# Stick-breaking attention on one core: logarithm sums over a high and a low part, scores asked for two pairs of heads ahead, pooling samples written as whole rows

## The chip, the cores and the metric

The kernel runs on one core of one Trainium2 chip, as one program. The metric is the device time of one execution in microseconds (us); lower is better. Six engines matter here: TensorE for matrix products (PE, and PEld for its weight loads), VectorE (DVE), ScalarE (ACT), GpSimd (POOL), SyncE (SP, which only issues transfers), and 16 DMA engines that all queues share.

## What is computed

One inference step of a two-layer hybrid decoder, for a prompt of 512 tokens and 8 single-token samples, all in float32. Each layer is a feed-forward half step, a mixing step and a second feed-forward half step. The change touches only the mixing step of the first layer: stick-breaking attention of 8 heads of 64 and a pooling mixer of 4 channel groups.

```python
z = einsum('bqhd,bkhd->bhqk', qb, kb) * scale + bias
log_1m = where(mask, log_sigmoid(-z), 0.0)
log_w = log_sigmoid(z) + cumsum(log_1m, axis=3, reverse=True) - log_1m
w = where(mask, exp(log_w), 0.0)
out = einsum('bhqk,bkhd->bqhd', w, vb)
```

The samples attend in the same way to 512 cached keys and values each, read through a page table. The pooling mixer also returns, for each sample, its last 15 pooling inputs (`pool_sample`).

## The kernel before

Stages follow each other: `in0`, `out0` (feed-forward), `evin` (the projection of layer 0), attention, `evout` (its output projection), and so on. All engines run their own queue in program order and meet only at semaphores. The order of the work is written out by hand, one function per engine: `even_sp`, `even_pe`, `even_act`, `even_dve`, `even_pool`.

Float32 weights are not multiplied as float32. Each weight block is split into a high part `WH` (fp32r, by ACT, line 2140) and a low part `WL` (by DVE, line 2318), and three fp32r products take the place of one float32 product. Attention before the change uses plain float32 products instead.

For one head `h` the causal scores are kept transposed and packed: block j (of 4) holds keys 128j to 128j+127 and queries from 128j on, so the blocks are 512, 384, 256 and 128 columns wide (`LEN`), 1280 in all (`CAUSAL`). A head goes through these steps:

- `score` (PE, 685): 4 products into PSUM; the two heads of a pair use the two halves of the array rows. `PS[0]` has room for one block of each head of a pair.
- `biased` (DVE, 1056): scale and bias, PSUM into `ZS`; POOL then masks the diagonal block (1223).
- `sized` (DVE, 1096) or, for heads 0 and 1, an Abs on ACT (890): |z| into `SP`.
- `decay` (ACT, 892 and 898): exp(-|z|). `log` (ACT, 902): ln(1 + that). Between Exp and Ln ACT loads a table (2164).
- `softplus` (DVE, 1062): max(z, 0) + logarithm.
- `sums` (PE, 791 and 794): for each key block i, one product with the triangle `TRI` and one with `ONES` for each later block, 10 products a head; the float32 products show in the trace as two instructions each. `PS[1]` has two buffers.
- `log_weights` (DVE, 1069): z minus the sum. `weights` (ACT, 906): exp. `values` (PE, 809): the product with V for a pair; ACT and DVE then make the high and low part of the result (952, 1100).

The main loop runs over pairs t = 0 to 3. On PE, before the change, one period takes the blocks of the scores of pair t+1 in turn with the sums of head 2t (`scores`, `sums`), then `values(t-1)` among them, then `values_past(t)` (660, the cached values of two samples), then `ada_step("head", 2t)` (1960, blocks of the modulation matrix), the sums of head 2t+1, and `ada_step("head", 2t+1)`. Before the loop, PE runs `sums_past` (715, 718), `scores_of_one` (the scores of head 1) and `ada_step("start", 0)`. `side(i, half)` puts small work between the products of the last `evin` units i = 22 to 27: `scores_past`, `pooled`, `turn_past` and the scores of head 0 (`first_scores`).

SP loads the weight blocks (1916), the modulation blocks `AW` for each `ada_step` (633, each once its buffer has been used), and writes the outputs K, the pooling rows and V (625 to 629). POOL issues the cached pages (1231): the values of samples 2q and 2q+1 once `values_past(q-1)` has used the two buffers `KV`.

## Time and profile before

| | |
|---|---|
| median of 3 runs | 2427.94 us (2426.88 to 2428.55) |
| the profiled execution | 2428.46 us, its span 2426.8 us |
| PE busy | 2382.4 us, 98% of the span |
| DVE, ACT, POOL busy | 1241.0, 994.5, 114.9 us |
| attention: from 563.15 us (`sums_past`) to 654.26 us (first product of `evout`) | 91.1 us |
| the chain that ended last, shares | PE 88%, DVE 5%, ACT 3%, DMA 2% |

The span is what the trace covers; 1.7 us of the execution lie around it. Times in the rows count from the span's start. In the timeline a row is start, duration, engine, line, operation, output and inputs, shapes and a count of merged instructions; "[1.05 <-DVE ZN L1164]" is the time for which the engine was idle before it and what ended that. A matmul's duration includes the way through the array, so the price of a product in a dense row of products is the distance from one start to the next.

### The profile page before, as it was taken

Reading aid. Unit: us, or ns where it says so; the run is one execution under the profiler, and the core shown is the slowest. Engines: PE = TensorE matmul, PEld = TensorE weight load, DVE = VectorE, ACT = ScalarE, POOL = GpSimd, SP = SyncE. Lnnn points to the kernel's source line nnn. Section 1 sums busy time; section 2 is a strip of 40 time slices with the busy share of each in tenths; the row PEclk is TensorE's granted clock in tenths of the full one; section 3 lists DMA queues with packets and bytes.
Section 4 is the critical chain, followed back from the end, with each engine's and each line's share of the span. In section 5 each row is a group of like instructions: output and inputs, shape, how many; then the busy total and the mean of one; then the engine's idle time right before and its main releaser. Section 6 shows DMA issues by size and latency. Waiting matters only on the chain.

```text
span 2426.8 us, 43808 instructions
## 1 busy us (share of the span) xinstructions
PE 2382.4 (98%) x18802; PEld 2183.8 (90%) x18802; DVE 1241.0 (51%) x1725; ACT 994.5 (41%) x1399; POOL 114.9 (5%) x232
## 2 busy tenths in 40 slices
PE   6999999999999999999999999999999999999998
PEld 5999999965699999999999999887777999999998
DVE  5533246755576333357523347755554758633245
ACT  5422235635456222346422245533223546522243
POOL 0000000122100000000000000012222100000000
PEclk9999999999999999999999999999999999999999
DMA  8555345785537653565754255544545456642254
GB/s 308 180 183 183 124 149 179 252 211 139 190 113 228 215 173 95 188 206 175 261 184 156 83 168 189 188 153 165 170 165 165 136 177 182 206 126 88 87 179 155
DMA packets 122660, 417.10 MB, mean 172 GB/s; under 512 B 23387, under 2 KB 27611, under 8 KB 122211
## 3 DMA queue, kind: packets, MB, share of 16 engines
q1 hardware_dynamic: 88962, 301.92, 39.1%
q10 hardware_dynamic: 18144, 62.03, 7.1%
q0 software_dynamic: 15360, 50.34, 6.3%
q8 instruction: 149, 2.44, 0.4%
q14 instruction: 45, 0.36, 0.0%
HBM read 390.84 MB, written 23.41 MB: 171 GB/s over the span
## 4 chain that ended last, share of the span: by engine, by line
PE 88%; DVE 5%; ACT 3%; DMA 2%; issue 1%; SPq 0%; ACTq 0%; POOL 0%; DVEq 0%; POOLq 0%
PE PS L2026 70%; PE PS L1425 3%; PE PS L1960 2%; DVE WL L2318 2%; PE PS L1990 2%; PE PS L1355 1%; ACT WH L2140 1%; DMA AFIRST<-in_w_ada 1%; PE PS L791 1%; PE PS L1309 1%; PE PS L1340 1%; PE PS L1350 1%; PE PS L753 1%; DMA RAW<-in_w_out 1%; PE PS L1321 1%
## 5 line engine op out<-in xcount | busy, mean ns | idle before, releaser
L2318 DVE TENSOR_TENSOR WL<-RAW,WH 128x1024 fp32r<-128x1024 f32 (+1 forms) x478 | 633.0, 1325 | 647.9 <-ACT WH L2140 647.2
L2026 PE MATMUL PS<-HH,WH 128*128 128x260 f32 x3432 | 796.6, 285 | 3.2 <-DVE QKVS L1119 1.8
L2026 PE MATMUL PS<-HH,WL 128*128 128x260 f32 x3432 | 786.5, 283 | 0.0
L2026 PE MATMUL PS<-HL,WH 128*128 128x260 f32 x3368 | 769.6, 283 | 0.0
L2140 ACT ACTIVATE WH<-RAW 128x1024 fp32r<-128x1024 f32 (+1 forms) x478 | 542.2, 1135 | 425.4 <-PE PS L2026 267.0
L2026 PEld LDWEIGHTS PS<-HH,WH 128*128 128x128 f32 x3432 | 569.9, 188 | 25.4 <-issue 16.8
L2026 PEld LDWEIGHTS PS<-HH,WL 128*128 128x128 f32 x3432 | 569.4, 188 | 0.0
L2026 PEld LDWEIGHTS PS<-HL,WH 128*128 128x128 f32 x3368 | 557.0, 188 | 0.6 <-issue 0.2
L2026 PE MATMUL PS<-GH,WH 128*128 128x260 f32 x1408 | 386.4, 285 | 0.9 <-DVE WL L2318 0.8
L2026 PE MATMUL PS<-GL,WH 128*128 128x260 f32 x1408 | 384.2, 283 | 0.0
L2026 PE MATMUL PS<-GH,WL 128*128 128x260 f32 x1408 | 383.5, 283 | 0.0
L2026 PEld LDWEIGHTS PS<-GH,WH 128*128 128x128 f32 x1408 | 259.0, 188 | 3.4 <-issue 1.8
L2026 PEld LDWEIGHTS PS<-GL,WH 128*128 128x128 f32 x1408 | 258.9, 188 | 0.2
L2026 PEld LDWEIGHTS PS<-GH,WL 128*128 128x128 f32 x1408 | 259.1, 188 | 0.0
L2263 ACT ACTIVATE GH<-SQ 128x260 fp32r<-128x260 f32 (+1 forms) x118 | 62.3, 528 | 376.5 <-DVE SQ L2488 376.5
L2488 DVE TENSOR_TENSOR SQ<-SG,PS 128x260 f32<-128x260 f32 (+1 forms) x118 | 65.6, 556 | 166.6 <-PE PS L2026 165.8
L2260 ACT ACTIVATE SG<-PS 128x260 f32<-128x260 f32 (+1 forms) x118 | 57.6, 488 | 217.3 <-PE PS L2026 215.6
L2477 DVE TENSOR_TENSOR GL<-SQ,GH 128x260 fp32r<-128x260 f32 (+1 forms) x118 | 66.3, 562 | 57.6 <-ACT GH L2263 56.9
L2026 PE MATMUL PS<-OGL,WH 128*128 128x260 f32 x256 | 69.6, 282 | 0.0
L1960 PE MATMUL PS<-AW,CSP 128*32 128x256 f32 x1024 | 67.0, 383 | 0.0
L1879 POOL DMA_DIRECT2D SR<-in_ret_past x32 | 18.2, 570 | 952.5 <-DVE WL L2318 929.0
L1960 PEld LDWEIGHTS PS<-AW,CSP 128*32 128x32 f32 x1024 | 30.4, 109 | 23.0 <-issue 2.3
(340 smaller groups left out, 2317.5 us busy)
## 6 DMA issues: line engine op xcount, KB each, us to landing
RAW<-in_w_in SPq DMA_DIRECT2D x236, 512.0 KB, 3.7
RAW<-in_w_out SPq DMA_DIRECT2D x120, 704.0 KB, 4.0
AW<-in_w_ada ACTq DMA_DIRECT2D x114, 512.0 KB, 5.5
RAW<-in_w_odd SPq DMA_DIRECT2D x60, 512.0 KB, 3.7
RAW<-in_w_odout SPq DMA_DIRECT2D x30, 512.0 KB, 3.9
RAW<-in_w_even SPq DMA_DIRECT2D x28, 512.0 KB, 4.0
KV<-in_v_pages POOLq DMA_DIRECT2D x32, 256.0 KB, 4.8
SR<-in_ret_past POOLq DMA_DIRECT2D x32, 256.0 KB, 4.0
```

Source lines behind the costliest of these rows:

```text
L753: last = nc.tensor.matmul(PS[tt // 2][:, tt % 2, :], src[k][:, tt // 2, (tt % 2) * P:(tt % 2 + 1) * P], w[:, w0:w0 + RV], start=(j + kk + ...
L791: last = nc.tensor.matmul(PS[1][:, i % 2, 0:LEN[i]], TRI[:], SP[h % 4][:, OFF[i]:OFF[i] + LEN[i]], start=True, stop=(i == 3))
L1425: last = nc.tensor.matmul(PS[tt // 2 if full else 0][:, tt % 2, :], src[k][:, tt // 2, (tt % 2) * P:(tt % 2 + 1) * P], w[:, w0:w0 + RV], s ...
L1960: last = nc.tensor.matmul(ADAP[CG * j:CG * j + CG, int(g == 1), 0:2 * P], CSP[:, k, :], w[:, 2 * P * j:2 * P * j + 2 * P], start=(k == 0), ...
L1990: last = nc.tensor.matmul(ps[:, x, 0:HT], w[:, k * P:(k + 1) * P], src[k][:, x, :], start=(start and k == 0), stop=(stop and k == KC - 1))
L2026: last = nc.tensor.matmul(ps[:, x, 0:HT], w[:, k * P:(k + 1) * P], src[k0 + k][:, x, :], start=(begin and t == 0), stop=(end and t == 2))
L2140: nc.scalar.activation(parts(p)[0], RAW[:, from_:from_ + w], ACT.Copy).then_inc(hi_done, 1)
L2260: nc.scalar.activation(SG[:, s, hs], PS[0][:, hs, 0:HT], ACT.Silu).then_inc(gate_evac, 1)
L2263: nc.scalar.activation(GH[:, r // 2, hs], G32[:, s, hs], ACT.Copy).then_inc(gh_done, 1)
L2318: nc.vector.tensor_tensor(low_, RAW[:, from_:from_ + w], high_.bitcast(F32), ALU.subtract).then_inc(lo_done, 1)
L2477: nc.vector.tensor_tensor(GL[:, r // 2, hs], G32[:, r // 2 % 2, hs], GH[:, r // 2, hs].bitcast(F32), ALU.subtract).then_inc(gl_done, 1)
L2488: nc.vector.tensor_tensor(G32[:, s, hs], SG[:, s, hs], PS[1][:, hs, 0:HT], ALU.mult).then_inc(up_evac, 1)
```

## The change

All of it is in the attention of layer 0 and the outputs written beside it.

```diff
-        ZS / SP: four buffers each, used by h % 4
+        ZS = [ZQ[h % 4] ...]; SP = [SQ5[n] for n in (0, 1, 2, 3, 0, 4, 2, 3)]   # five buffers
+        SPL: the same memory as SP, fp32r;  SPH: two buffers, fp32r;  TRIR, ONESR: TRI and ONES as fp32r
 even_sp
-                if i == 3:
+                if i == 0:                      # before the first evout load
                     sp.wait_ge(ev_act, EV_FULL)
                     sp.wait_ge(ev_dve, EV_FULL)
                     for dst, src in ((k_t[:, 0:4 * SEQ], KP[:]), (k_t[:, 4 * SEQ:4 * SEQ + 32], QKVS[:, 4:8, :]),
-                                     (pool_p, UP[:, :, SEQ + 1:SEQ + 16]), (pool_n, US[:, :, :, 1:16])):
-                        sp.dma_start(dst, src).then_inc(out_done, 16)
+                                     (pool_p, UP[:, :, SEQ + 1:SEQ + 16]), (pool_n, US[:])):
+                        sp.dma_start(dst, src).then_inc(pool_out, 16)
 even_pe
+            POOLED_AT = {(23, 4): 0, (24, 2): 1, (24, 4): 2, (25, 2): 3}
+            SCORES_AT = {(25, 3): 0, (25, 4): 1, (26, 1): 2, (26, 2): 3, (26, 3): 4, (26, 4): 5}
+            def side(i, quarter):               # quarter: after each of the 4 products of a unit
+                ... scores_past at (22..25, 4), turn_past at (26, 2)
+                if (i, quarter) in SCORES_AT:
+                    first_scores(SCORES_AT[i, quarter])      # heads 0 and 1, one PSUM buffer
+                if (i, quarter) == (27, 3):
+                    sums_past()
             def sums(h, i):
                 if i == 0:
-                    pe.wait_ge(sp_done, h + 1)
+                    pe.wait_ge(spl_done, h + 1)
-                last = nc.tensor.matmul(..., TRI[:], SP[h % 4][...])
-                for j in range(i + 1, 4):
-                    last = nc.tensor.matmul(..., ONES[:], SP[h % 4][...])
+                for j in range(i, 4):
+                    w = TRIR if j == i else ONESR
+                    for x, part in enumerate((SPH[h % 2], SPL[h])):
+                        last = nc.tensor.matmul(..., w[:], part[...])
-            sums_past()
-            scores_of_one()
+            for j in range(4):
+                scores(1, j)                    # pair 1
+                sums(0, j)
             ada_step("start", 0)
             for t in range(PAIRS):
-                scores(t + 1, 0); sums(2 * t, 0); scores(t + 1, 1); values(t - 1); sums(2 * t, 1)
-                scores(t + 1, 2); sums(2 * t, 2); [t == 2: gather(0)]; scores(t + 1, 3); sums(2 * t, 3)
-                if t < 3: values_past(t)
-                ada_step("head", 2 * t)
-                sums(2 * t + 1, 0..3)
-                if t == 3: values_past(3)
-                ada_step("head", 2 * t + 1)
-            gather(1)
-            values(3)
+                if t:
+                    sums(2 * t, 0..3)
+                values_past(t)
+                ada_step("head", 2 * t)
+                sums(2 * t + 1, 0..3)
+                if t == 1: gather(0)
+                scores(t + 2, 0..3)
+                ada_step("head", 2 * t + 1)
+                if t == 3: gather(1)
+                values(t)
 even_act
+            def high_part(h):
+                act.wait_ge(sp_done, h + 1)
+                nc.scalar.activation(SPH[h % 2], SP[h], ACT.Copy).then_inc(sph_done, 1)
+            # decay(h): only the Exp; |z| now comes from sized(h) on DVE for every head
+            # evin i == 26: Exp table, TRIR, ONESR, pooled_samples, the past's Abs and Exp, decay(0), Ln table, logs
+            # evin i == 27: high_part(0), Exp table; then value_rows(0), decay(1), value_rows(1..3), ZW, log(1), high_part(1)
             for t in range(PAIRS):
+                if t == 0: weights(0)
+                if t < 3: decay(2t+2), decay(2t+3), table, log(2t+2), log(2t+3), table
+                if t: outputs(t - 1), weights(2t)
+                weights(2t+1)
+                if t < 3: high_part(2t+2), high_part(2t+3)
 even_dve
+            def low_part(h):
+                dve.wait_ge(sph_done, h + 1)
+                nc.vector.tensor_tensor(SPL[h], SP[h], SPH[h % 2].bitcast(F32), ALU.subtract).then_inc(spl_done, 1)
+            scored(1, 0); VSR; memset; log_weights(0, 0); scored(1, 1); log_weights(0, 1); softplus(1)
+            scored(1, 2); log_weights(0, 2); scored(1, 3); log_weights(0, 3); sized(2); low_part(1); sized(3)
             for t in range(PAIRS):
+                if t: low_part(2t); log_weights(2t, 0..3); low_part(2t+1)
+                if t == 1: copy_past(0)
+                log_weights(2t+1, 0..3)
                 ada_evac("head", 2 * t)
+                if t: low(t - 1)
+                if t == 1: copy_turned(0)
+                scored(t + 2, 0..3)
+                softplus(2t+2); softplus(2t+3); sized(2t+4); sized(2t+5)
                 ada_evac("head", 2 * t + 1)
 outputs
-            "pool_n": (P, 4, NS, BUF)
+            "pool_n": (P, 4, NS, 16)            # the host drops the first of the 16 columns
```

The loops of `even_act` and `even_dve` are shown in shortened form; what they replace stands in the functions above.

## Rows read from the trace of the kernel before

**Rows 1.** The page: span, and the chain that ended last, by engine
```profile
span 2426.8 us, 43808 instructions
PE 88%; DVE 5%; ACT 3%; DMA 2%; issue 1%; SPq 0%; ACTq 0%; POOL 0%; DVEq 0%; POOLq 0%
```
**Rows 2.** Windows: length, busy PE, PEld, DVE, ACT, POOL, granted clock, DMA share, GB/s
```profile
580.00:600.00 20.00, 18.90 (x114) 10.32 (x112) 13.56 (x21) 10.56 (x9) 6.40 (x16) 1.00 0.61 211
600.00:620.00 20.00, 18.45 (x100) 9.71 (x96) 14.42 (x23) 10.75 (x9) 5.71 (x14) 1.00 0.46 159
```
**Rows 3.** Timeline of PE, late `evin` and attention
```profile
527.82 3.61 PE L646 MATMUL PS<-KV,QBM 128*16 128x512 f32 x16
...
563.15 1.13 PE L715 MATMUL PS<-ZN,TRI 128*128 128x512 f32 x2 [1.05 <-DVE ZN L1164]
...
577.67 3.18 PE L660 MATMUL PS<-KV,ZW 128*8 128x512 f32 x14
...
583.13 1.12 PE L791 MATMUL PS<-SB,TRI 128*128 128x512 f32 x2 [0.99 <-DVE SB L1062]
...
587.92 1.07 PE L1960 MATMUL PS<-AW,CSP 128*32 128x256 f32 x16
588.92 1.13 PE L685 MATMUL PS<-QP,KP 64*128 64x512 f32 x4
589.98 1.13 PE L791 MATMUL PS<-SC,TRI 128*128 128x512 f32 x2
...
610.08 1.10 PE L791 MATMUL PS<-SA,TRI 128*128 128x512 f32 x2
```
**Rows 4.** The chain in order of time (start, us, what), end of attention
```profile
652.05 2.21 PE PS L809 x16
654.26 3.25 PE PS L2026 x24
```
**Rows 5.** Timeline of PE: fp32r products of 512 and of 260 columns
```profile
556.36 0.39 PE L753 MATMUL PS<-WH,HH 128*128 128x512 f32 x1
556.59 0.40 PE L753 MATMUL PS<-WH,HL 128*128 128x512 f32 x1
...
654.54 0.28 PE L2026 MATMUL PS<-OHB,WL 128*128 128x260 f32 x1
654.66 0.28 PE L2026 MATMUL PS<-OHB,WH 128*128 128x260 f32 x1
```
**Rows 6.** Timeline of DVE: biased, sized, softplus, log_weights
```profile
571.05 0.75 DVE L1056 TENSOR_SCALAR ZC<-PS,BIAS 128x512 f32<-128x512 f32 x1 [0.84 <-DMA out_v_s<-VSR]
571.72 0.74 DVE L1056 TENSOR_SCALAR ZD<-PS,BIAS 128x512 f32<-128x512 f32 x1
...
580.20 1.48 DVE L1096 SCALAR_TENSOR_TENSOR SD<-ZD 128x1280 f32<-128x1280 f32 x1
581.60 1.48 DVE L1062 SCALAR_TENSOR_TENSOR SB<-ZB,SB 128x1280 f32<-128x1280 f32 x1
585.59 0.69 DVE L1069 TENSOR_TENSOR ZB<-ZB,PS 128x512 f32<-128x512 f32 x1 [2.52 <-PE PS L794]
```
**Rows 7.** Timeline of ACT: log, table load, weights
```profile
585.56 1.35 ACT L902 ACTIVATE SD<-SD,ONES 128x1280 f32<-128x1280 f32 x1
586.93 1.28 ACT L2164 ACT_TABLE_LOAD   x1
588.22 1.27 ACT L906 ACTIVATE SA<-ZA 128x1280 f32<-128x1280 f32 x1
```
**Rows 8.** Timeline of PE near the start of the program
```profile
22.78 4.36 PE L1960 MATMUL PS<-AFIRST,CSP 128*32 128x256 f32 x48 [2.54 <-DMA AFIRST<-in_w_ada]
```
**Rows 9.** Windows of one us there, columns as in rows 2
```profile
23.00:24.00 1.00, 1.00 (x12) 0.40 (x8) 0.00 (x0) 0.00 (x0) 0.00 (x0) 0.50 1.03 414
26.00:27.00 1.00, 1.00 (x20) 0.36 (x12) 0.00 (x0) 0.00 (x0) 0.00 (x0) 0.99 1.01 401
```
**Rows 10.** DMA issues between 510 and 550 us: KB each, median us to landing
```profile
KV<-in_v_pages POOLq DMA_DIRECT2D x8, 256.0 KB, 16.5
```
**Rows 11.** Line 633 (AW loads), 625 to 645 us
```profile
DMA to landing us min/median/max: 3.5/4.3/8.1
```
**Rows 12.** Timeline of POOL: the last K pages of q = 2, then V pages of q = 3
```profile
521.66 0.54 POOL L1231 DMA_DIRECT2D KV<-in_k_pages  x1 [0.61 <-issue]
...
626.79 0.55 POOL L1231 DMA_DIRECT2D KV<-in_v_pages  x1 [4.57 <-issue]
...
635.13 0.54 POOL L1231 DMA_DIRECT2D KV<-in_v_pages  x1 [0.61 <-issue]
```

More of the change, by code:

```diff
@@ L834, in even_pe @@
                     sums(2 * t + 1, i)
+                if t == 1:
+                    gather(0)
+                for j in range(4):
+                    scores(t + 2, j)
+                ada_step("head", 2 * t + 1)
                 if t == 3:
-                    values_past(3)
-                ada_step("head", 2 * t + 1)
-            gather(1)
-            values(3)
+                    gather(1)
+                values(t)
             def chunk_ready(k):
@@ L947, in even_act @@
             table(EXP_SET)
+            high_part(1)
             def outputs(t):
@@ L1166, in even_dve @@
                     softplus(0)
+                    ada_evac("evin", i)
+                if i == 27:
+                    first_scored(1, 2)
+                    first_scored(1, 3)
+                    ada_evac("evin", i)
+                    sized(1)
+                    low_part(0)
             dve.wait_ge(zn_pe, 2)
+            nc.vector.tensor_tensor(ZN[:, 0, :], ZN[:, 0, :], PS[2][:, 0, :], ALU.subtract).then_inc(zn_dve, 1)
             dve.wait_ge(unit_done, POS["evin"] + len(EV))
[L1169 removed]
@@ L1170, in even_dve @@
-            scored_one()
+            scored(1, 0)
             nc.vector.tensor_copy(VSR[0:NS, :], PS[3][0:NS, 1, :]).then_inc(vs_ok, 1)
             dve.wait_ge(vs_ok, 1)
-            nc.vector.memset(PS[3][:, 1, :], 0.0).then_inc(pz_ok, 1)
-            for t in range(PAIRS):
-                if t == 2:
+            nc.vector.memset(PS[3][:, 1, :], 0.0).then_inc(z_zero, 1)
+            log_weights(0, 0)
+            scored(1, 1)
+            log_weights(0, 1)
+            softplus(1)
+            scored(1, 2)
@@ L1176, in even_dve @@
+            log_weights(0, 2)
+            scored(1, 3)
+            log_weights(0, 3)
+            sized(2)
+            low_part(1)
+            sized(3)
+            for t in range(PAIRS):
+                if t:
+                    low_part(2 * t)
+                    for i in range(4):
+                        log_weights(2 * t, i)
+                    low_part(2 * t + 1)
+                if t == 1:
                     copy_past(0)
-                scored(t + 1, 0)
-                log_weights(2 * t, 0)
@@ L1179, in even_dve @@
-                scored(t + 1, 1)
+                for i in range(4):
+                    log_weights(2 * t + 1, i)
+                ada_evac("head", 2 * t)
                 if t:
                     low(t - 1)
-                log_weights(2 * t, 1)
-                scored(t + 1, 2)
-                scored(t + 1, 3)
-                if t == 2:
+                if t == 1:
                     copy_turned(0)
-                sized(t + 1, 0)
-                log_weights(2 * t, 2)
-                log_weights(2 * t, 3)
@@ L1190, in even_dve @@
-                sized(t + 1, 1)
-                if t == 0:
-                    softplus(1)
-                ada_evac("head", 2 * t)
-                for i in range(2):
-                    log_weights(2 * t + 1, i)
-                if t < 3:
-                    softplus(2 * t + 2)
-                for i in range(2, 4):
-                    log_weights(2 * t + 1, i)
-                if t < 3:
-                    softplus(2 * t + 3)
+                for j in range(4):
+                    scored(t + 2, j)
@@ L1202, in even_dve @@
+                softplus(2 * t + 2)
+                softplus(2 * t + 3)
+                sized(2 * t + 4)
+                sized(2 * t + 5)
                 ada_evac("head", 2 * t + 1)
```

285 lines of the change are left out of this document (146 added, 139 removed).

## The prediction

> **What bounds the kernel now.** I read the page first: the chain that ended last is PE for 88% [rows 1], so the whole is a queue of products, and a stage gets shorter only where PE's work shrinks or its waits do. The change lies in one stage, from 563.15 us, the first product of `sums_past` [rows 3], to 654.26 us, the first product of `evout` [rows 4]: 91.1 us. There the windows show PE busy 18.9 and 18.5 us of 20, DVE 13.6 and 14.4, ACT 10.6 and 10.8, at a granted clock of 1.00 [rows 2]. So PE bounds it, but with only 1.1 to 1.5 us of 20 free, and DVE is two thirds full. The timeline of PE says how: scores of the next pair and sums of this head alternate, and each hides the other's evacuation by DVE.
>
> **Prices.** One head's float32 sums last from 583.13 to 587.92, 4.79 us [rows 3]. An fp32r product of 512 columns costs 556.59 - 556.36 = 0.23 us, one of 260 costs 654.66 - 654.54 = 0.12 us [rows 5], so 384 take 0.175. No row has an fp32r product of 128 columns. Bounds: a quarter of the 512 price, 0.06, and 0.213, the price of the same columns in float32 (a block of 512 float32 columns takes about 0.85, in two instructions). I take 0.12, since below 260 columns each product still brings its own load of 128 weights and no row has such a pair faster. Twice each product, block i = 0 costs 2 x (0.23 + 0.175 + 0.12 + 0.12) = 1.29, i = 1 0.83, i = 2 0.48, i = 3 0.24: 2.84 us of products. Since the two PSUM buffers make blocks 2 and 3 wait for `log_weights` (0.69 for 512 columns and 1.48 for a pass of 1280 [rows 6], so 1.03 ns a column: 0.56, 0.42, 0.29 for the others), a head takes PE 3.2 us and DVE is through 3.65 us after its start. At 0.06 these are 2.75 and 3.25, at 0.213 3.75 and 4.2.
> The Trainium skill (TensorE: Matmul & The Clock Gate, Back-to-back issue gap) gives about 81 ns a product for a stream of load and product at 128 columns. No run here shows it; by it a head would be some 0.3 us shorter, 2 us over seven heads, an estimate.
>
> A DVE pass over 1280 columns is 1.48 us, the next one starts 581.60 - 580.20 = 1.40 after it [rows 6]. `low_part` is such a pass, new for eight heads; `sized` is new for heads 0 and 1, where ACT did it. `high_part` is an ACT pass like the weights, 1.27; the Abs of two heads goes. A table is 1.28 [rows 7]. A block of 512 scores costs PE 589.98 - 588.92 = 1.06 for a pair or a single head [rows 3], and DVE 0.67 + 0.74 for a pair [rows 6].
>
> **The change laid out, at full clock.** On paper PE saves 8 x 1.6 = 12.8 us. I follow who waits for whom.
> - In `evin` only the order changes. Head 1's scores (2.55) and `sums_past` (2.4) move in ahead of the last products; each of the six groups waits for DVE to clear one shared buffer, some 0.9 us in all. `evin` ends at 567.9; the old kernel was through with the same work (5.4 us of products after 563.15) at 568.5.
> - Next PE alternates the scores of pair 1 with the sums of head 0 as before, but DVE carries VSR, the memset and `softplus(1)` among them: sums(0, 3) ends at 576.9. Then start, `values_past(0)` to 581.3. The AW blocks of head 0 can be issued only when start's are used (577.4 and 577.9), and now follow within 3.5 us; at a landing of 4.3 us and more [rows 11] they come at 582.2 and 582.6, so PE is at sums(1) at 583.1. The old kernel was there at 583.13: nothing gained.
> - t = 0: sums(1) to 586.3, DVE to 586.8. Now the scores of pair 2 stand alone: PE 1.06 + 0.85 + 0.65 + 0.45 and DVE 1.42 + 1.15 + 0.88 + 0.60 strictly in turn through one pair of buffers, 7.4 us, DVE until 593.7. DVE then has softplus, softplus, sized, sized and low_part(2) before PE may begin sums(2): 4 x 1.40 + 1.5 = 7.1. PE has one `ada_step` and `values(0)` to fill that, 3.3 us. **PE stands idle some 4.5 us**, until 600.9. The old kernel began sums(2) at 589.98 [rows 3].
> - t = 1: sums(2) 3.2, `values_past` and head 2 4.35 (577.67 to 583.13 less 0.99 of waiting, and the rest of the start block, in the old trace [rows 3]), sums(3) 3.2, gather 0.55, scored 7.4, the same four passes 5.6, the modulation 0.4, low_part(4) 1.5: sums(4) at 627.3, with 5.5 us idle. The old period was 610.08 - 589.98 = 20.1 us [rows 3], this one is 26.4.
> - t = 2 has no scores ahead: 3.2 + 4.35 + 3.2, then head 5 (its AW blocks again one step late), weights(5), high_part(6), low_part(6): sums(6) at 643.5.
> - t = 3: 3.2; the pages of q = 3 are issued in 8 steps, 8.3 us from first to last [rows 12], after values_past(2) at 633.9, and at 4 to 5 us of transfer land at 647.4, so 0.7 us of waiting; `values_past(3)` and head 6 to 651.8; sums(7) to 655.0. Head 7's blocks were issued after head 6's and land 4 to 5 us later [rows 11]: 657.0. Then the copies, gather(1), and `values(3)` 2.2 [rows 4]: **661.1 against 654.26, +6.8 us**.
> So the saved products do not shorten the path, because DVE, not PE, is last at each of the two turns of the loop.
>
> The scores that ran between the sums hid DVE's evacuations; that cover is gone. The output writes go ahead of the first `evout` load on SP and meet the K pages for `scores_past(2)`, the last of which is issued at 521.66 [rows 12] and used from 527.82 [rows 3]: at some 4 us of transfer 2 us to spare. 1 MB more at some 300 GB/s (between the 211 and 414 of rows at hand [rows 2, 9]) is 3.5 us, so 0 to 1.5 us; I take 0.7. Whole rows of 16 take away 4096 small pieces of 60 bytes; the V pages issued behind them took 16.5 us to land [rows 10], but are not used before 577 us, so this gains nothing by itself. It is needed, since DVE and ACT now wait for this write (`pool_out`) from about 555 us; issued at 516 us, it is done. `low_part` and `high_part` cost time only where I counted them.
>
> **The clock.** After 2.54 us without a product PE's clock was granted at 0.50, that is 1.2 GHz, until about 26 us, and at 2.4 GHz again from there [rows 8, 9]. The two gaps above are longer than that one. I price each at half of a stretch as long as that slow one, 1.7 us, and 0.9 for the thin stretch around 572 to 577: 4.3 in all, between 0 and 8.
> The Trainium skill (TensorE: Matmul & The Clock Gate, the HAM clock gate) says that idleness halves this clock and that sustained work gives it back; the trace agrees in the rows just named, and it speaks against this change, which opens gaps on PE.
>
> **Sum.** 2428.46 (the profiled execution; 0.5 above the median) + 6.8 + 0.7 + 4.3 = 2440.3; against the median of the runs, 2439.8.
>
> **Rivals.**
> - Slower still: 128-column fp32r products cost 0.213, as float32 ones do. Seven heads on the path, 0.55 each: +3.9, 2443.7. Nothing in the trace shows fp32r at 128 columns, so nothing excludes it. Chance 0.17.
> - No change: the clock stays at 2.4 GHz and 128 columns cost 0.06 (-3.2): 2427.9 + 6.8 - 3.2, that is 2431.5, up to 2433. Against it speaks the slow stretch at 23 us [rows 9]. Chance 0.2.
> - Faster: PE keeps the lead. If DVE's four passes after the scores were ready before PE is through with head and values, the idle gaps go and the saved products count: 2427.9 - 8 x 1.6 = 2415. It decides at a DVE queue of 3.3 us between last score and low_part, where I read 7.1; or part of it, if my order of waits is wrong. Chance 0.1.
> - The change does not do what it says: the write of whole rows is still slow and DVE waits at 555 us. The old one held the pages behind it for up to 16.5 us [rows 10]; from 520 us on that ends before 540. Even then no cost; it is in no case of its own.
>
> **How the numbers follow.** The forecast, DVE-bound with some clock loss, 2433 to 2442, has 0.5; the slow products 0.17; a larger clock loss 0.03; within 0.2% 0.2; faster 0.1. 0.2% is 4.9 us, about what a measurement of this kernel tells from no change. Slower by more: 0.7. The range leaves out the faster case and the far end: 2430 to 2447.
>
> **What would show it.** In the profile after: PE idle 4 to 6 us before the first product of sums(2) and of sums(4), released by DVE's low part; a granted clock below 1.00 behind them; a head's sums 3.2 us dense; `evin`'s last unit ending near 568; the last values at 659 to 666. Wrong if PE's idle in attention is below 6 us in all, if sums take over 3.7 us, or if the stage ends before 654. DVE passes of much less than 1.4 us or a low part not last before the sums would upset it.

## The result

| | before | after |
|---|---|---|
| median | 2428.24 us (2426.88 to 2431.97, 4 runs) | 2453.59 us (2450.09 to 2455.56, 4 runs) |
| profiled execution, span | 2428.46, 2426.8 | 2450.09, 2448.5 |

The ratio is 1.0098, 95% interval 1.0082 to 1.0114: slower by 24 us. 2439.8 was predicted, with a range of 2430 to 2447; the sign was right, the time lies 6.6 us outside the range. The case nearest to it, a larger clock loss, had been given a chance of 0.03.

The page of the kernel after, span and the chain that ended last:
```profile
span 2448.5 us, 43830 instructions
...
PE 86%; DVE 6%; DMA 3%; ACT 3%; issue 2%; SPq 1%; POOLq 0%; POOL 0%; ACTq 0%; DVEq 0%
```
PE's share of the chain fell from 88% [rows 1]: waits took its place. Windows of the kernel after (length, busy PE, PEld, DVE, ACT, POOL, granted clock, DMA share, GB/s):
```profile
520.00:540.00 20.00, 17.44 (x63) 9.14 (x63) 2.96 (x4) 3.12 (x4) 7.66 (x15) 0.91 0.85 294
580.00:600.00 20.00, 15.66 (x92) 6.71 (x90) 12.63 (x17) 11.46 (x10) 7.71 (x16) 0.84 0.73 238
600.00:620.00 20.00, 15.50 (x104) 10.42 (x100) 11.17 (x16) 11.11 (x10) 2.17 (x4) 0.82 0.26 91
620.00:640.00 20.00, 11.34 (x44) 6.35 (x43) 12.44 (x17) 9.44 (x9) 5.55 (x12) 0.69 0.27 93
```
Where PE was busy 18.9 and 18.5 us of 20 at a clock of 1.00 [rows 2], it is now busy 11 to 16 us at 0.69 to 0.84 from 580 us on. DVE is no fuller than before: no engine is the bound by its load. The timeline of PE (start, duration, ..., idle time before and what ended it):
```profile
527.60 5.31 PE L654 MATMUL PS<-KV,QBM 128*16 128x512 f32 x16 [2.56 <-DMA KV<-in_k_pages]
...
584.95 0.50 PE L811 MATMUL PS<-SHB,TRIR 128*128 128x512 f32 x1
...
586.10 0.22 PE L811 MATMUL PS<-SHB,ONESR 128*128 128x128 f32 x1
586.16 0.27 PE L811 MATMUL PS<-SXL,ONESR 128*128 128x128 f32 x1
586.27 0.39 PE L811 MATMUL PS<-SHB,TRIR 128*128 128x384 f32 x1
...
588.25 1.13 PE L693 MATMUL PS<-QP,KP 64*128 64x512 f32 x4
590.95 0.92 PE L693 MATMUL PS<-QP,KP 64*128 64x384 f32 x4 [1.57 <-DVE ZB L1085]
593.10 0.81 PE L693 MATMUL PS<-QP,KP 64*128 64x256 f32 x4 [1.23 <-DVE ZB L1085]
594.86 0.80 PE L693 MATMUL PS<-QP,KP 64*128 64x128 f32 x4 [0.95 <-DVE ZB L1085]
...
605.76 0.79 PE L811 MATMUL PS<-SHA,TRIR 128*128 128x512 f32 x1 [4.50 <-DVE SCL L1105]
...
636.48 0.79 PE L811 MATMUL PS<-SHA,TRIR 128*128 128x512 f32 x1 [4.91 <-DVE SAL L1105]
...
654.62 0.50 PE L811 MATMUL PS<-SHA,TRIR 128*128 128x512 f32 x1 [1.05 <-DVE SCL L1105]
...
660.21 2.32 PE L668 MATMUL PS<-KV,ZW 128*8 128x512 f32 x10 [2.21 <-DMA KV<-in_v_pages]
```
and the chain in order of time, end of attention:
```profile
671.63 3.82 PE PS L827 x16
675.45 3.24 PE PS L2067 x24
```
The same places before are 583.13 and 610.08 [rows 3] and 652.05 and 654.26 [rows 4]. From sums(1) to the first product of `evout` it was 654.26 - 583.13 = 71.1 us; it is 675.4 - 585.0 = 90.4. The +21.7 us of the spans are: -2.85 up to the first scores of past keys (508.78 before, 505.93 after; in `evin`, which the change does not touch there, and in the 19 traces of all kernels this point lies anywhere between 505.8 and 509.2), +4.3 at the K pages (2.56 of waiting, then 16 products in 5.31 us in place of 3.61 [rows 3]), +0.35 up to sums(1), +19.4 from there to `evout`, +0.45 behind.

Idle gaps of 4.50 and 4.91 us before sums(2) and sums(4), both released by the low part, were predicted as 4.5 and 5.5. Between 505 and 690 us of this execution the granted clock is at half (0.50, 1.2 GHz) for 34.1 us: 528.7 to 532.1, 593.6 to 600.4, 603.8 to 610.6, 624.3 to 631.1, 634.5 to 641.4 and 672.1 to 675.5; before the change it is never at half there. One window of 1 us there, columns as above:
```profile
606.00:607.00 1.00, 1.00 (x3) 0.81 (x4) 0.00 (x0) 0.99 (x2) 0.00 (x0) 0.50 0.00 0
```
What the slow clock does behind PE is seen on DVE:
```profile
597.74 1.57 DVE L1101 SCALAR_TENSOR_TENSOR SD<-ZD,SD 128x1280 f32<-128x1280 f32 x1
601.41 1.49 DVE L1095 SCALAR_TENSOR_TENSOR SA<-ZA 128x1280 f32<-128x1280 f32 x1 [2.10 <-PE PS L827]
602.82 1.48 DVE L1095 SCALAR_TENSOR_TENSOR SB<-ZB 128x1280 f32<-128x1280 f32 x1
604.22 1.48 DVE L1105 TENSOR_TENSOR SCL<-SC,SHA 128x1280 fp32r<-128x1280 f32 x1
...
631.72 1.49 DVE L1095 SCALAR_TENSOR_TENSOR SC<-ZC 128x1280 f32<-128x1280 f32 x1 [1.25 <-PE PS L827]
```
`sized(4)` overwrites the memory that `values(0)` reads, so it waits for it, and the low part that PE will wait for is queued behind both; `sized(6)` waits for `values(1)` in the same way. PE's slow products thus came back to PE through DVE's queue. The prediction had not followed this wait.

### The profile page after: what moved, and what is told of

It reads as the page before. It is cut to its first block, busy times and chain, and to the rows that moved or that the text cites. A ratio compares the mean times of both kernels' runs of the same rounds, so it can differ in the third digit from the quotient of the medians.

```text
span 2448.5 us, 43830 instructions
## 1 busy us (share of the span) xinstructions
PE 2382.0 (97%) x18802; PEld 2185.9 (89%) x18802; DVE 1255.1 (51%) x1735; ACT 1003.8 (41%) x1407; POOL 117.3 (5%) x232
## 4 chain that ended last, share of the span: by engine, by line
PE 86%; DVE 6%; DMA 3%; ACT 3%; issue 2%; SPq 1%; POOLq 0%; POOL 0%; ACTq 0%; DVEq 0%
PE PS L2067 70%; PE PS L1465 3%; PE PS L2001 2%; DVE WL L2359 2%; PE PS L2031 1%; PE PS L1395 1%; DMA RAW<-in_w_in 1%; ACT WH L2181 1%; PE PS L1349 1%; PE PS L811 1%; PE PS L1380 1%; PE PS L1390 1%; PE PS L1361 1%; ACT Y L2232 1%; PE PS L693 1%
## 5 line engine op out<-in xcount | busy, mean ns | idle before, releaser
L1919 POOL DMA_DIRECT2D SR<-in_ret_past x32 | 18.3, 571 | 954.4 <-DVE WL L2359 930.9
```

## The experiments

All ratios are against the kernel before on the same chip, with 95% intervals; differences between two kernels are taken from their ratios, 0.001 being 2.4 us. "Half clock" is the time at 0.50 between 505 and 690 us, in the one execution of each kernel that has a trace. The theory at first was: the loss beyond the prediction is the clock, the K pages and DVE's order. The rivals: the split costs by itself, or the order does.

**Products thrown away into the gaps.** On the kernel after; the products' results are not used.
```diff
+ scores(t, j), t >= 2, j > 0: wait for the log weights; one float32 product of 512 columns
+ behind values(0), values(1): 5 and 6 such products;  before values_past(3): 2
```


> The changed kernel with float32 products of ONES and K, whose result is thrown away, put into PE's waits of the attention loop: one of 0.86 us ahead of blocks 1 to 3 of the scores of pairs 2 and 3, five and six after values(0) and values(1), two before values_past(3). No other wait changes. Theory (the granted clock is what made the change cost more than my 6.8 us of waiting): the clock stays at 1.00 from 590 to 660 us, sums(2) and sums(4) last 3.2 us and not 5.2, values(0) and values(1) 2.3 and not 3.8 to 4.2, and the kernel gets 8 to 12 us faster than the changed one, to 12 to 16 us above the kernel before. Rival (the excess is DVE's queue and late transfers, the low clock falls on idle time): the clock stays high and the time moves by less than 2 us, or gets worse by the filler's own time.


Measured: 2448.84, 1.0068 (1.0056 to 1.0080). Half clock fell from 34.1 to 13.7 us, sums(1) to `evout` from 90.4 to 85.3. That is 7 us for 20 us less at half clock, a little less than the 8 to 12 that the theory gave and far more than the rival's 2. Window and timelines of PE and DVE:
```profile
590.00:640.00 50.00, 48.20 (x262) 23.59 (x261) 33.25 (x46) 26.88 (x23) 13.91 (x30) 1.00 0.37 127
```
```profile
604.07 0.51 PE L818 MATMUL PS<-SHA,TRIR 128*128 128x512 f32 x1
...
630.99 0.50 PE L818 MATMUL PS<-SHA,TRIR 128*128 128x512 f32 x1 [0.31 <-DVE SAL L1117]
...
647.30 0.50 PE L818 MATMUL PS<-SHA,TRIR 128*128 128x512 f32 x1 [1.04 <-DVE SCL L1117]
...
663.98 0.64 PE L2013 MATMUL PS<-AW,CSP 128*32 128x256 f32 x8 [2.53 <-DMA AW<-in_w_ada]
```
```profile
599.73 1.48 DVE L1107 SCALAR_TENSOR_TENSOR SA<-ZA 128x1280 f32<-128x1280 f32 x1
...
602.53 1.48 DVE L1117 TENSOR_TENSOR SCL<-SC,SHA 128x1280 fp32r<-128x1280 f32 x1
```
This run separates the clock from the rest, stretch by stretch (us; sums(1) is at 585.81 here, `evout` at 671.08):

| from, to | predicted without clock loss | after | gaps filled |
|---|---|---|---|
| sums(1), sums(2) | 17.8 | 20.8 | 18.3 |
| sums(2), sums(4) | 26.4 | 30.7 | 26.9 |
| sums(4), sums(6) | 16.2 | 18.1 | 16.3 |
| sums(6), `evout` | 17.6 | 20.8 | 23.8 |

Up to sums(6) the clock stayed at 1.00 and DVE's low part still came last, so the added products delayed nothing: the schedule comes out within 1.1 us of the predicted one, 8.2 us less than after the change, and `sized(4)` and `sized(6)` follow the softplus without the waits of 2.10 and 1.25 us. In the last stretch two products of the filling, late AW blocks (2.53 us) and 6.8 us at half clock took 3.0 us of it back.

**The outputs in their old place**, otherwise the kernel after.
```diff
-                if i == 0:     (K and pooling outputs)
+                if i == 3:
```


> The changed kernel with only the K and pooling writes put back on SP behind the first three evout loads (i == 3); whole rows kept. Theory (these writes hold up the K pages): PE's wait of 2.56 us ahead of scores_past(2) and the slow clock after it go, 4.3 us less up to the pooled products, and the kernel is 3 to 5 us faster than the changed one. The write still has to land before DVE clears the scores of head 1 at 555 us: issued at 531 us in whole rows it does, so no new wait. Rival (the pages are late for another reason, POOL's own issue): the wait stays, 0 us. Rival 2: pool_out lands late and DVE waits at 555 us, up to 5 us slower.


Measured: 2448.38, 1.0075 (1.0062 to 1.0088), 5.6 us less, though the interval overlaps with that of the kernel after (1.0082 to 1.0114). The wait at the K pages is gone, and with it the slow stretch behind it; the clock is at half as long as before the edit, now for 6.8 us from 574.0.

**The next low part ahead of the sizes**, so that it no longer stands behind the wait for `values`.
```diff
-                if t: low_part(2 * t)              (start of the period)
                 softplus(2t+2); softplus(2t+3)
+                if t < 3: low_part(2 * t + 2)
                 sized(2t+4); sized(2t+5)
```


> The changed kernel with DVE's low_part(2t+2) moved from behind the two sized passes to ahead of them, nothing else. Theory (DVE's queue between the last score and low_part is what PE waits for): the sums of heads 2 and 4 start 2.8 us earlier, PE's idle time before them falls from 4.5 and 4.9 us to below 2.5, the clock drops less, and the kernel is 6 to 12 us faster than the changed one. Rival (PE is held by the AW blocks, V pages or values, the DVE queue is hidden): below 2 us.


Measured: 2442.65, 1.0045 (1.0032 to 1.0058): this one edit gives back half of the loss, 12.9 us, where 6 to 12 had been expected. The gaps of 4.5 and 4.9 us are gone, 1.46 and 1.73 us came up inside the sums, where log_weights now stand behind the sizes; sums(1) to `evout` 82.7.

**Float32 sums in the new order.** The high and low parts are left out.
```diff
-  TRIR, ONESR with SPH and SPL;  high_part, low_part
+  TRI, ONES with SP
```


> The changed kernel without the high and low parts: the sums as float32 products straight from softplus, as before the change, while the order (scores two pairs ahead, all at once) stays. It leaves high_part and low_part out, so it computes the same thing as the kernel before. Theory (the new order is what costs, the split gives a little back): a head's sums take 4.8 us and not 3.2 (+1.6 for six or seven heads on the path, about +10), DVE's low_part is gone (-1.5 at three or four places, -5), PE's idle gaps shrink by 1.5 us each and the clock drops less (-2 to -4): within 4 us of the changed kernel, so still 20 us or more above the kernel before. Rival (the split is what costs, through two more passes on the chain): 10 us or more faster than the changed kernel.


Measured: 2443.7, 1.0048 (1.0035 to 1.0061): 12 us less than with the split. The theory (within 4 us of the changed kernel) falls, and the rival's 10 us or more holds: in this order the split costs half of the loss. The other half is there without any split.

**Scores between the sums of the odd head**, on the kernel after.
```diff
                 for i in range(4):
                     sums(2 * t + 1, i)
+                    scores(t + 2, i)        (and scored(t + 2, i) behind log_weights(2t+1, i))
```


> Edit: in each pair the scores of the pair two ahead stand between the sums of the odd head (sums(2t+1,i), scores(t+2,i)) and their biased copies between its log weights, in place of one block of eight behind them. Theory A (the loss is made by the serial run scores, biased, softplus, high and low part before the next pair's sums, with TensorE idle and then at half clock behind it): the scored block of 8 us, with its 1.57, 1.23 and 0.95 us of idle TensorE time, comes into the 8 us of sums and subtractions, softplus of the next pair starts 4 to 6 us sooner a pair, and with it falls part of the 13.7 us of half-clock stretches: 2440 +- 4, from sums(1) to evout 80 us instead of 90.4. Theory B (VectorE is what sets the pair's time, its instructions only change places): 2452 to 2456, unchanged.


Measured: 2447.56, 1.0078 (1.0065 to 1.0091). Between the theories, less than A gave: the low part still stood behind `sized`, and PE waited 4.50 us for it at 601.92.

**The softplus and the low part early**, on the kernel after.
```diff
+                if t: ... low_part(2t+1); softplus(2t+2); softplus(2t+3); low_part(2t+2)   (before log_weights(2t+1, .))
```


> Edit: softplus of both heads of the next pair and the low part of its first head are issued by VectorE right behind the low part of the odd head, before that head's log weights, and ScalarE makes the first high part right behind the weights of the even head. Theory A (the 4.5 and 4.9 us of idle TensorE time before sums(2) and sums(4) are the chain softplus, high part, low part issued too late): both waits go, 9.4 us, and with them two half-clock stretches of 6.8 us, worth 3.4 us each if TensorE is the bound there: 2442 +- 4. Theory B (the logs of ScalarE are not ready earlier, VectorE then waits for them in front of the log weights and the wait moves inside the odd head's sums): 2450 or more, with the idle time in front of the sums' second product and behind.


Measured: 2447.37, 1.0076 (1.0063 to 1.0089), a time between the theories. The mechanism is the one that B names: DVE now waited 2.59 us for the high part ahead of the odd head's log weights, twice. The waits of PE before sums(2) and sums(4) are gone, but it waits inside the sums: 4.05 and 3.05 us in odd heads, 1.47 and 1.88 us in even ones.

**The split alone, in the old order.** On the kernel before: parts, fp32r constants and whole rows; scores one pair ahead, outputs as before.
```diff
+  ACT: weights(2t); high_part(2t+2); weights(2t+1); high_part(2t+3)
+  DVE: softplus(2t+2); ...; softplus(2t+3); low_part(2t+2);  next period: low_part(2t+3) before its log weights
```


> Edit, on the kernel before: only the high and low parts with the sums over them (the constants rounded once, high part on ScalarE behind the weights, low part on VectorE), and whole rows for the pooling samples; scores one pair ahead and all other orders as before, the outputs too. Theory A (the order of the change is what costs; the split frees 8 x 2.4 = 19 us of TensorE in a stage where TensorE is busy nearly all the time, against 8 x 1.35 us of VectorE and as much of ScalarE): 2418 to 2430. Theory B (the split itself costs some 12 us, as the kernel after against the same order with float32 sums did, 2453.6 against 2443.7 - here about 10): 2438 to 2442, with TensorE idle in front of each head's first sum and its clock at half behind.


Measured: 2439.30, 1.0047 (1.0034 to 1.0059). Theory A falls: the freed time of PE turned into waits. Its timeline of PE:
```profile
584.93 0.80 PE L803 MATMUL PS<-SHB,TRIR 128*128 128x512 f32 x1 [3.87 <-DVE SBL L1095]
...
594.41 0.51 PE L803 MATMUL PS<-SHA,TRIR 128*128 128x512 f32 x1 [2.10 <-DVE SCL L1095]
...
608.90 0.51 PE L803 MATMUL PS<-SHB,TRIR 128*128 128x512 f32 x1 [1.93 <-DVE SDL L1095]
...
641.46 0.80 PE L803 MATMUL PS<-SHA,TRIR 128*128 128x512 f32 x1 [4.58 <-DVE SCL L1095]
```
Every head's first sum waits for its low part (the other three of heads 1 to 7: 1.63, 0.51 and 0.78 us). The expectation's 2.4 us saved per head was too much: a dense head takes 3.3 us for 4.79. Softplus, high part and low part are 1.48 + 1.27 + 1.48 = 4.2 us between the logarithm and the first sum; without the split the softplus alone was.

**Three edits together**: outputs late, softplus and low part early, scores between the sums.
```diff
 SP    outputs at i == 3
 PE    sums(2t+1, i); scores(t+2, i)
 DVE   log_weights(2t, .); low_part(2t+1); softplus(2t+2); softplus(2t+3); low_part(2t+2); log_weights(2t+1, i) with scored(t+2, i)
```


> Edit: both edits of the two runs before (scores between the odd head's sums; softplus and first low part early) and the four outputs back in their old place behind the third of the last stage's loads. Theory A (three causes that add: serial block, late chain, K pages 4.3 us): 2432 +- 5, K-page wait gone, from sums(1) to evout under 76 us. Theory B (VectorE or ScalarE is the bound once TensorE's waits are gone): 2442 to 2448 with VectorE over 85% busy from 585 to 660 us.


Measured: 2440.39, 1.0049 (1.0036 to 1.0062); sums(1) to `evout` 664.2 - 581.7 = 82.5. Neither theory: better than the parts alone, but far from 76, since the wait of DVE for the high part and that for `values` are both still there (2.59 us twice; 4.74 us for `values(1)`). DVE is busy 61% from 585 to 660 us, so it isn't the bound by its load, as B had it.

**The order alone.** On the kernel after: float32 sums, outputs late.
```diff
-  TRIR, ONESR with SPH and SPL;  outputs at i == 0
+  TRI, ONES with SP;  outputs at i == 3
```


> Edit, on the kernel after: the sums in float32 over the whole logs as before (no high and low parts), and the four outputs back behind the third of the last stage's loads; what is left of the change is the new order, the new homes of the tiles and the whole rows. Theory A (order and K pages add: the same kernel with early outputs had ratio 1.0048, 11.7 us, of which the K pages are 4.3): 1.0030 +- 0.001, 2435. Theory B (with float32 sums TensorE is busy enough to hide what the outputs delay): 1.0045 to 1.005, as with early outputs. Theory C (the order alone is free, all its cost was the outputs' and the disturbed runs'): 1.000 to 1.001.


Measured: 2441.28, 1.0049 (1.0035 to 1.0062); with the outputs early it was 1.0048. Theory B: with float32 sums the outputs' place made no difference. The cost of the order is in its timeline:
```profile
591.02 0.92 PE L693 MATMUL PS<-QP,KP 64*128 64x384 f32 x4 [1.57 <-DVE ZB L1079]
593.17 1.23 PE L693 MATMUL PS<-QP,KP 64*128 64x256 f32 x4 [1.23 <-DVE ZB L1079]
595.36 0.80 PE L693 MATMUL PS<-QP,KP 64*128 64x128 f32 x4 [0.96 <-DVE ZB L1079]
```
3.76 us of idle PE in each of two pairs, because scores alone go in turn with DVE through one pair of buffers; in each, 6.8 us at half clock follow.

**Products thrown away, old order.** On the split in the old order, 17 such products in front of the heads' first sums.
```diff
             def sums(h, i):
+                if i == 0 and h: wait lw_done >= 4h - 1; (4, 2, 2, 2, 1, 5, 1)[h - 1] float32 products of 512 columns
                 pe.wait_ge(spl_done, h + 1)
```


> Edit, on the kernel before with the split in the old order (2439.3, 1.0047): thrown-away float32 products, 17 of 512 columns in all, into a free half of a PSUM bank in front of each head's first sum, where TensorE waited 3.9, 2.1, 1.9, 1.6, 0.5, 4.6 and 0.8 us for the low part; each takes 0.9 to 1 us at full clock, so most fit into the waits. Theory A (what half clock took, 20.5 us of it, is 7 to 10 us of the 11.6): clock back at full from 575 to 660 us, ratio 1.0015 to 1.0025, 2432 to 2434. Theory B (the wait for the low part is what costs, the clock only fills time that TensorE would wait anyway): 1.004 to 1.005.


Measured: 2440.12, 1.0047 (1.0034 to 1.0061), the same as without them, though half clock fell from 20.5 to 3.4 us. From `sums_past` to `evout` its trace has 96.6 us in place of 100.3, but it reached `sums_past` 4.7 us later: 2.7 of that lie ahead of the first scores of past keys, where the two kernels don't differ, and 2.0 behind them, with a wait of 2.46 us for a K page where the other had 1.82. So it doesn't price the clock.

**The low part first and the outputs late together.**
```diff
 SP    outputs at i == 3
 DVE   softplus(2t+2); softplus(2t+3); low_part(2t+2); sized(2t+4); sized(2t+5)
```


> Edit, on the kernel after: the low part of the next even head right behind the two softplus (alone 2442.7, ratio 1.0045 against 1.0098: 12.9 us less), and the four outputs in their old place (alone 1.0075: 5.6 us less). Theory A (they act in different stretches, 520 to 530 and 600 to 640 us, and add): 1.0022 +- 0.001, 2433.5. Theory B (earlier K pages only move the wait to the V pages, or the clock falls elsewhere): 1.004 to 1.005.


Measured: 2442.67, 1.0057 (1.0044 to 1.0071). The two do not add. PE no longer waits for the K pages, but it waits 2.69 us for the V pages of values_past(3) (2.23 with the low part first alone), and the clock is at half for 30.7 us. Why the gain of the late outputs is lost here stays open.

**Whole rows alone**, on the kernel before.
```diff
-  (pool_n, US[:, :, :, 1:16])
+  (pool_n, US[:])
```


> Edit, on the kernel before: only the pooling samples stored as whole rows of 16 instead of 15 of 16, everything else as it was. Theory A (the output of 512 descriptors of 15 words becomes one long run a partition, on a queue that nobody waits for in this stretch): 0.9995 to 1.0005. Theory B (fewer descriptors free the queues for the loads behind them): 0.998 to 0.9992. Theory C (a contiguous store is faster and meets the K pages): 1.001.


Measured: 2428.66, 1.0002 (0.9993 to 1.0011): no change of the time, theory A. But the transfers did change. The store had 4096 pieces of 60 bytes (not 512, as the expectation has it), and the V pages issued behind it, which took 16.5 us to land [rows 10], now take 6.1; packets under 512 bytes between 510 and 550 us fall from 4718 to 1142. The DMA issues of 510 to 550 us:
```profile
KV<-in_v_pages POOLq DMA_DIRECT2D x8, 256.0 KB, 6.1
```
Nobody uses these pages before 577 us, so the time doesn't show it.

**The queues laid out so that nobody waits.** On the kernel after: outputs late, scores between the sums, and
```diff
 DVE  log_weights(2t, .); low_part(2t+1)
+     sized(2t+2); sized(2t+3)                  (beside values_past; before: sized(2t+4), sized(2t+5) a period earlier)
      log_weights(2t+1, i) with scored(t+2, i); softplus(2t+2); softplus(2t+3)
+     low_part(2t+2)
 ACT
+     outputs(t-1); weights(2t); decays; logs; weights(2t+1); high_part(2t+2); high_part(2t+3)
```


> Edit, on the kernel after: outputs in their old place, scores between the sums of the odd head, and VectorE's and ScalarE's order laid out so that no step waits for the other engine: the sizes of the next pair behind the low part of the odd head (beside the products with the past values) instead of behind the softplus, where they waited for values(t); the two softplus and the next low part behind the scored blocks; on ScalarE the decays and logs between weights(2t) and weights(2t+1). Theory A (the chain is what costs: VectorE has 19 us of work a pair, TensorE 17.5, and nothing else need wait): from sums(1) to evout 72 +- 3 us, where after had 90.4 and before 71.1, ratio 0.9985 to 1.002. Theory B (TensorE then still runs a third of the time at half clock, as in the other variants, and that holds the rest): 1.003 to 1.005, with VectorE waiting for TensorE.


Measured: 2434.78, 1.0023 (1.0012 to 1.0034). The split and the scores two pairs ahead are all there, and three quarters of the loss are gone. The timeline of PE:
```profile
583.53 0.50 PE L811 MATMUL PS<-SHB,TRIR 128*128 128x512 f32 x1
...
619.72 0.79 PE L811 MATMUL PS<-SHA,TRIR 128*128 128x512 f32 x1 [2.26 <-DVE SAL L1102]
...
637.01 1.11 PE L827 MATMUL PS<-SA,VP 128*64 128x512 f32 x1 [2.72 <-ACT SB L917]
...
657.75 0.39 PE L2064 MATMUL PS<-OHB,WH 128*128 128x260 f32 x1
```
657.75 - 583.53 = 74.2 us, as theory A has it (after 90.4, before 71.1), in an execution 2 us below the median; the whole kernel's 1.0023 is just above A's 1.002. Half clock is 13.7 us, one of its stretches (592.3 to 595.7) behind three gaps of only 0.61 to 0.69 us among the scores.

**The order with scores between the sums, float32**: the order alone plus the interleaving.
```diff
                 for i in range(4):
                     sums(2 * t + 1, i)
+                    scores(t + 2, i)
```


> Edit, on the kernel after: float32 sums (no parts), outputs in their old place (this was 1.0049), and the scores between the sums of the odd head. Theory A (in the order alone the cost is the ping-pong of scores and biased copies, 3.76 us of idle TensorE in two pairs, and the half clock behind it): 1.001 to 1.0025. Theory B (VectorE's order is what costs, and the wait moves to the sums): 1.004 to 1.005.


Measured: 2432.44, 1.0016 (1.0007 to 1.0024), theory A. The turn-taking of scores and DVE, with the half clock that follows it, was 8 us of the order's 12: half clock fell from 13.7 us to nothing.

**Low part first, with thrown-away products.**
```diff
 DVE   softplus(2t+3); low_part(2t+2); sized(2t+4)
+PE    one product between score blocks, 5 and 6 behind values(0) and values(1), 2 before values_past(3)
```


> Edit, on the kernel after: the low part early (alone 1.0045), and the thrown-away products between the score blocks, behind values(0) and values(1) and before the last products with the past values (alone 1.0068). Theory A (clock and chain are two costs, the filling gave 7.3 us on its own and gives most of it here too): 1.002 to 1.003. Theory B (the clock's cost was that of slow products inside the chain; with the chain shorter the filling only stands in TensorE's way, as in the old order): 1.004 to 1.006.


Measured: 2445.22, 1.0063 (1.0051 to 1.0075), against 1.0045 (1.0032 to 1.0058) without them: theory B or slightly worse, no gain in any case. Half clock fell from 27.3 to 13.7 us and the time did not; the blocks of 4 to 5 us that the products take stood in PE's way, and head 7's AW blocks came 3.19 us late. Filling shows what the clock costs only where PE had really nothing to do.

**Three more steps of the queues**, on the balanced kernel.
```diff
 DVE   low(t-1), copy_turned: behind low_part(2t+2);   t == 2: sized(6), sized(7) ahead of low_part(5)
 ACT   t == 2: high_part(6) ahead of weights(5)
```


> Edit, on e13: the split of the outputs' rest and the turned past values (0.85 us) behind the next low part instead of ahead of the softplus; in the third pair the sizes ahead of the odd head's low part, and ScalarE's high part of head 6 ahead of the weights of head 5. Theory A (these steps are on the chain into sums(4) and sums(6)): 0.85 and 1.2 to 2.5 us off, ratio 1.001 to 1.0015, from sums(1) to evout 71.5 +- 1 us. Theory B (what is taken from one chain comes back in the next, values(2) later by 1.3 us, or at half clock): 1.002 to 1.003.


Measured: 2431.68 (2429.93 to 2437.96, 12 runs), 1.0012 (1.0002 to 1.0022). It is the nearest to the kernel before; no kernel with the change beat that. The ratio is theory A's; its stage of 71.5 us wasn't seen, as the one trace is of a slow execution (2437.59 us, half clock 30.7 us, stage 77.7 us). These 12 executions also price the clock: the granted clock over the span was 0.991 in three of them, at 2437.6, 2437.8 and 2438.0 us, and 0.994 to 0.996 in nine, at 2429.9 to 2435.2. The line through all twelve falls 1.6 us for each 0.001. As 1 us at half clock lowers the mean by 0.5 / 2430 = 0.0002, a us at half clock costs 0.33 us. The balanced kernel's 7 executions give 0.9 us for each 0.001, or 0.19. The same line through the 4 to 8 executions of other kernels scatters from below zero to 0.6. This is how the executions of one program lie together, not an edit.

**The outputs early, on the balanced kernel.**
```diff
-                if i == 3:
+                if i == 0:     (K and pooling outputs)
```


> Edit, on e13: only the four outputs where the change has them, ahead of the first of the last stage's loads. Theory A (they hold up the K pages: 2.5 us of wait before the third scores of past keys and 1.8 us at half clock): 1.0040 to 1.0046, 4 to 5.6 us more than e13. Theory B (as with float32 sums, 1.0048 and 1.0049, the page wait is time that a later wait gives back): 1.002 to 1.003.


Measured: 2437.54, 1.0035 (1.0023 to 1.0047): 0.0012, some 3 us, between the theories and within the intervals of the two. In the traces the way from the first scores of past keys to sums(1) is 80.8 us against 76.1. PE again waits at the K pages:
```profile
529.19 5.31 PE L654 MATMUL PS<-KV,QBM 128*16 128x512 f32 x16 [3.54 <-DMA KV<-in_k_pages]
```
In the profiles of all eight kernels with the outputs early (the change, and those of its variants that leave the outputs there) this wait for the third pair of samples' pages is there, 2.1 to 3.5 us; in none with the outputs late (two of those, both with the split in the old order, waited 1.8 and 2.5 us for the fourth pair's instead, others at most 0.5). The DMA issues of 505 to 535 us, KB each and median us from issue to landing, first before, then after the change:
```profile
KV<-in_k_pages POOLq DMA_DIRECT2D x8, 256.0 KB, 3.6
```
```profile
KV<-in_k_pages POOLq DMA_DIRECT2D x8, 256.0 KB, 7.0
```

## Why the prediction was right, and where it failed

- **PE bounds the old kernel, and the saved products do not shorten the path**: right. The split alone in the old order costs 11 us where, by the prediction's prices, it frees some 13 of PE.
- **128-column products**: 586.16 - 586.10 = 0.06 us for the high part and 0.11 for the low part with the next load, where 0.12 was taken; a dense head takes 588.25 - 584.95 = 3.3 us against 3.2. The rival of slow products is out. Each product has its own weight load. The mean of the two, 0.085, agrees with the 81 ns of the Trainium skill (TensorE: Matmul & The Clock Gate, Back-to-back issue gap).
- **The schedule at full clock**: right. Its two gaps were right to 0.6 us (4.50 and 4.91 measured), and so were their cause and releaser. That the lengths came out is in part luck: DVE's low part was 3.0 us later than predicted before sums(2), but PE's own slow work before the gap had grown by nearly as much. The better test is the run with the gaps filled, which at full clock keeps this schedule to 1.1 us up to sums(6). (The items given for the period of t = 1 add up to 26.2, not 26.4.) The schedule was 6.8 us longer than before; that DVE's four passes and low part are what is late is confirmed by the balanced kernel, which reorders them, interleaves the scores and puts the outputs late.
- **The clock term, 4.3 us, is the step that failed.** It priced two gaps and one thin stretch, 1.7 us each or less. The trace has six slow stretches, 34.1 us. In the rows the same work took longer by 1.5 to 1.9 us each time: sums(2) and sums(4) 5.2 us for 3.3, values(0) 3.8, values(1) 4.2 and values(3) 3.9 for 2.3, the K scores 1.7 more; 10.5 us in all. The run with the gaps filled says nearly the same: 8.2 us up to sums(6), and with 1.6 in values(3) and 1.7 at the K scores 11.5 us, where 4.3 were taken. From the executions' own spread it would be 34.1 x 0.33 = 11.3 us, or 6.5 by the lower price. The prediction looked at the long gaps only. The clock also fell at 593.6, among the scores, behind gaps of 1.57 and 1.23 us with short products between. The Trainium skill (TensorE: Matmul & The Clock Gate, A second HAM failure mode: psum-queue depth-cycling) describes this: groups that wait for their PSUM buffers in turn idle often enough to lose the clock. The trace agrees with the gaps just named, and so do two runs: with float32 sums half clock was 13.7 us while scores and DVE took turns and none once the scores stood between the sums. It belonged in the sum.
- **The missed wait**: `sized(4)` to `sized(7)` wait for `values(0)` and `values(1)` (2.10 and 1.25 us above), so a slow `values` delays the low part. With the gaps filled both waits are gone: at full clock they are nothing, and with the clock at half they made a loop, 3.4 of the 8.2 us. Moving the low part ahead gave 12.9 us (1.0098 to 1.0045), one of the two largest effects of a single edit; leaving out the split is the other. That is more than this wait, for it also takes the two sizes, 2.8 us of each period that the prediction had counted, out of the way.
- **K pages, 0.7 taken**: 2.56 us of wait and 1.7 of slow products in the trace, 4.3. By runs 5.6 us on the kernel after and 3 us on the balanced one, in both with intervals that overlap, and no gain with float32 sums or with the low part first: the wait is shown, its price in the whole is not. The estimate counted 1 MB where the four outputs are 1.3 MB, and took a delay from that alone: the landing of a page went from 3.6 to 7.0 us.
- **Whole rows**: no cost and no gain in time, as predicted, and for the reason given: the V pages land in 6.1 us in place of 16.5, and are not used so soon.

The spans add up: 78.0 us were predicted from sums(1) to `evout` without the clock term and 90.4 measured; the difference of 12.4 us is 8.2 + 1.6 of clock (the wait for `values` in it), 1.5 of V pages beyond the 0.7 taken, and 1.1 by which the filled run too is longer than predicted. The K pages are 3.6 us beyond their term, 1.7 of it clock. The 2.85 us before 506 us work the other way in that execution. The 8.2 us rest on one trace each of two kernels; for the last stretch, where the filling itself disturbed the order, the 1.6 us are read from the rows alone.

| kernel | ratio |
|---|---|
| whole rows alone | 1.0002 |
| split alone, old order | 1.0047 |
| new order alone, outputs early; late; late with scores between the sums | 1.0048; 1.0049; 1.0016 |
| both, outputs late | 1.0075 |
| both, outputs early: the change | 1.0098 |
| both, low part first; with outputs late too | 1.0045; 1.0057 |
| both, outputs early, gaps filled | 1.0068 |
| both, outputs late, queues balanced; and tuned | 1.0023; 1.0012 |

## What to carry to other kernels

Taking work from the engine that bounds a stage pays only if the steps that replace it are not on the chain into its next product; lay out each engine's queue by who waits for its result, and ask of each pass behind a wait what else is queued there. Once TensorE waits in a turn-taking stage, add up its short gaps too and price the half clock on all work behind them: here 0.2 to 0.4 us for each us at half clock, by the executions' spread and by the filling. A slow product costs twice where another engine waits for it. A transfer moved forward costs those that it now runs beside: read their landing times, not the bytes.

## What had not been expected of the hardware

- Executions of one program differ in how long the clock is at half: 0.991 to 0.996 over the span in one kernel, with 2438.0 to 2429.9 us. The kernel before stays between 0.996 and 0.999.
- The clock was lost behind gaps of 1.57 and 1.23 us as well as behind 4.50 us, and in the balanced kernel behind three of 0.61 to 0.69 us.
- Keeping PE busy in its gaps brought the granted clock back to 1.00 over 50 us and gained 7 us; with the low part first and in the old order the same gained nothing.
- 256 KB pages land in 3.6 us, and in 7.0 us with 1.3 MB of outputs issued just ahead of them on another queue. V pages behind 4096 pieces of 60 bytes land in 16.5 us, behind whole rows in 6.1.
